# Output turned and stored by channel tiles behind the last down products, and the last activation tile made between additions

## The chip, the core and the metric

The kernel runs on one core of one Trainium2 chip. The core has five engines, each with an instruction stream of its own, tied to the others by semaphores: TensorE (PE) multiplies and transposes, with its results in PSUM; VectorE (DVE), ScalarE (ACT) and GpSimd (POOL) work on elements; SyncE (SP) issues transfers, which 16 DMA engines carry out. The metric is the device time of one execution in microseconds; lower is better.

## The reference

One inference step of one decoder layer for a prompt of 1024 tokens and for 8 decoding sequences of one token. An attention branch and a recurrent branch are merged and projected; then comes a SwiGLU mixer with a causal convolution of width 3 along the tokens. The end of the layer is what matters here:

```python
def conv_ffn(h, w_up, conv_w, conv_b, w_down, buf):
    u, v = jnp.split(h @ w_up, 2, axis=-1)
    u_ext = jnp.concatenate([buf.astype(u.dtype), u], axis=1)
    y = conv_b
    for j in range(CONV_W):
        y = y + conv_w[j] * u_ext[:, j:j + t]
    return (jax.nn.silu(y) * v) @ w_down, u_ext[:, -(CONV_W - 1):]
...
    f_out, conv_new = conv_ffn(h2, lw['w_up'], lw['conv_w'], lw['conv_b'], lw['w_down'], conv_buf0)
    x = x + g2[:, None, :] * f_out
    return x, nsa_new + (s_hg, conv_new)
```

The model width is 1024, the hidden width of the mixer 2816. `x` is the output y_prompt (1024 x 1024) and y_sample (8 x 1024); `conv_new` holds the last inputs of the convolution.

## The kernel before

The residual stream `xT` lies in SBUF with channels on the partitions: KT = 8 channel tiles of 128, each with 1032 columns (1024 prompt tokens, 8 decode tokens). The columns are worked in three chunks c of CH = 344. Each matrix product is split into three of shorter numbers (`product`, lines 245 to 247: high by high, high by low, low by high), so every chunk of one weight tile is three instructions.

`stage_ffn` runs over FT = 22 hidden tiles f, two at a time in GR = 11 groups g. In `body(g, ...)` TensorE makes the up products of the two tiles (u into PSUM banks 0 to 2, v into 3 to 5) and then the down products of the group before: for each channel tile n and chunk c six products into bank 6 or 7 in turn. VectorE convolves, multiplies by v and splits the activation tile (`hidden`: three multiplications, L3025; a cast, L235; a subtraction, L240), and adds each down chunk to `xT` (L3060, with the decode columns apart, L3058, when c is 2). The semaphore `added` counts these additions, and TensorE waits for it before it writes a bank again. In a group, VectorE does both convolutions, then the 24 additions, then the activation tile 2g + 1. The last call, `body(GR, ...)`, has down products alone; its weights were loaded into the ring and split before. Before it TensorE waits for `a_ready`, which `hidden` gives.

Behind the last addition TensorE turns the tails (22 tiles of 10 columns, L2951) by groups of four, VectorE copies them (L3080), and SP stores them as p_cf and s_cf. Then `stage_output` runs in a block of its own: per tile t of 128 tokens TensorE turns eight 128 x 128 pieces of `xT` (L3099), VectorE copies one half of the channels (L3108) and ScalarE the other (L3116) into one of two buffers in the ring, and SP stores 128 whole rows of 4096 bytes (L3124). A copy waits until the store of two tiles before has landed. Nothing plans this order: each engine follows the order in which its instructions are written.

Of the kernel before, what the change touches and what calls it, by code (L numbers as in the profile page):

```python
# [13 lines left out]
ALU = mybir.AluOpType  # L14
# [3 lines left out]
P = 128  # L18
D = 1024
# [2769 lines left out]
def stage_ffn(nc, s, T, mix, up_weights, norm):  # L2789
# [30 lines left out]
    x = s.xT  # L2820

# [12 lines left out]
    with nc.Block() as block:  # L2834
        @block.sync
        def _(sp):
# [16 lines left out]
            sp.wait_ge(copied, (FT + 3) // 4)  # L2853
            sp.dma_start(T["p_cf"][0, 0], rows[0:2, :]).then_inc(out, 16)
            sp.dma_start(T["s_cf"][0, :, 1], rows[2:2 + NB, :]).then_inc(out, 16)
            sp.wait_ge(out, 32)
# [32 lines left out]
        def _(pe):  # L2889
# [3 lines left out]
            def body(g, par, up, down):  # L2893
# [34 lines left out]
                if down:  # L2928
                    weights = wd if up else wd_last
                    pe.wait_ge(dn_split, g)  # L2930
                    pe.wait_ge(a_ready, 2 * g)
                    for n in range(KT):
                        for c in range(3):
# [3 lines left out]
                            for e in range(2):  # L2937
                                last = product(pe, s.ps[6 + (3 * n + c) % 2][:, 0:CH], [w[:, e, n * P:(n + 1) * P] for w in weights],
                                               (aH[1 - par][:, e, cols], aL[1 - par][:, e, cols]), e == 0, e == 1)
# [5 lines left out]
            body(GR, 1, False, True)  # L2945

            pe.wait_ge(added, 24 * GR + 2)
            for f in range(FT):
                if f % 4 == 0 and f >= 8:
                    pe.wait_ge(copied, f // 4 - 1)  # L2950
                last = pe.transpose(s.ps[6 + f // 4 % 2][0:NB + 2, (f % 4) * P:(f % 4 + 1) * P],  # L2951
                                    tails[:, f * 10:(f + 1) * 10], s.ident[:, :])
                if f % 4 == 3 or f == FT - 1:
                    last.then_inc(turned, 1)
# [33 lines left out]

        @block.vector
        def _(v):  # L2990
# [26 lines left out]

            def hidden(f, h, par):

                whole, hi, lo = (t[par][:, h, :] for t in (a, aH, aL))  # L3020
                v.wait_ge(silu_done, f + 1)
                for c in range(3):
                    cols = slice(c * CH, (c + 1) * CH)
                    v.wait_ge(v_made, 3 * f + c + 1)
                    last = v.tensor_tensor(whole[:, cols], y[:, cols], s.ps[3 + c][:, 0:CH], ALU.mult)  # L3025
                    if c < 2:
                        last.then_inc(v_read, 1)
                ch.link(v, last)
                v.nop().then_inc(v_read, 1)
                ch.link(v, high(v, hi, whole))  # L3030
                low(v, lo, whole, hi).then_inc(a_ready, 1)

            def body(g, par, up, down, more=True):
# [28 lines left out]
                if up:  # L3062
                    hidden(2 * g + 1, 1, par)
# [12 lines left out]
            ch.link(v, v.tensor_tensor(x[:, :, SEQ:TOK], x[:, :, SEQ:TOK], dec, ALU.add))  # L3076
            for g in range((FT + 3) // 4):
                n = min(4, FT - 4 * g) * P
                v.wait_ge(turned, g + 1)
                v.tensor_copy(rows[0:NB + 2, 512 * g:512 * g + n], s.ps[6 + g % 2][0:NB + 2, 0:n]).then_inc(copied, 1)  # L3080


def stage_output(nc, s, T):

    y = [view(s.ring, 1024 * i, D) for i in range(2)]
    turned, done = s.sem("o_turned"), [s.sem("o_done_v"), s.sem("o_done_a")]
    sent = [s.sem(f"o_sent{i}") for i in range(2)]

    with nc.Block() as block:
        @block.tensor  # L3090
        def _(pe):
            for t in range(TT + 1):
                n = rows_of(t)
                for half in range(2):
                    g = 2 * t + half

                    wait(pe, done[half], t - 3)
                    for j in range(4):
                        last = pe.transpose(s.ps[g % 8][0:n, j * P:(j + 1) * P],  # L3099
# [166 lines left out]
```

## Time and profile before

| | us |
|---|---|
| median of 3 runs | 2311.18 (2309.67 to 2312.91) |
| the profiled execution | 2305.29 |
| its span | 2303.5 |
| TensorE busy | 2156.0, 94% of the span |
| VectorE busy | 1190.4, 52% |
| ScalarE busy | 660.4, 29% |
| GpSimd busy | 590.7, 26% |

The profile is one execution, and its times are counted from the start of the span. The granted clock is TensorE's: 1.00 is its level of 2.4 GHz, 0.50 that of 1.2 GHz; its mean here is 0.965. A duration of a product is from its start to its modelled end, and products overlap, so the distance between starts is what one costs in a row of them.

### The profile page before, as it was taken

Reading aid. Unit: us, or ns where it says so; the run is one execution under the profiler, and the core shown is the slowest. Engines: PE = TensorE matmul, PEld = TensorE weight load, DVE = VectorE, ACT = ScalarE, POOL = GpSimd, SP = SyncE. Lnnn points to the kernel's source line nnn. Section 1 sums busy time; section 2 is a strip of 40 time slices with the busy share of each in tenths; the row PEclk is TensorE's granted clock in tenths of the full one; section 3 lists DMA queues with packets and bytes.
Section 4 is the critical chain, followed back from the end, with each engine's and each line's share of the span. In section 5 each row is a group of like instructions: output and inputs, shape, how many; then the busy total and the mean of one; then the engine's idle time right before and its main releaser. Section 6 shows DMA issues by size and latency. Waiting matters only on the chain. (4 is left out here: it accounts for less than half of the span.)

```text
span 2303.5 us, 34296 instructions
## 1 busy us (share of the span) xinstructions
PE 2156.0 (94%) x13481; PEld 1967.1 (85%) x13481; DVE 1190.4 (52%) x2152; ACT 660.4 (29%) x1390; POOL 590.7 (26%) x367
## 2 busy tenths in 40 slices
PE   8999997988869999987999999999999999999996
PEld 3798785666656799987999999899999999999996
DVE  5773465888857167763110333565445444445444
ACT  3332464776744034431111212331111101110100
POOL 0112113444631155541000114422221202221200
PEclk9999897999979999988999999999999999999998
DMA  9021452000026312211333443221111111111101
GB/s 363 25 77 34 130 177 88 1 1 1 1 79 229 115 28 57 57 47 48 87 87 83 149 136 86 73 57 56 56 37 54 39 51 41 52 41 48 45 19 76
DMA packets 168405, 168.83 MB, mean 73 GB/s; under 512 B 10178, under 2 KB 147811, under 8 KB 162932
## 3 DMA queue, kind: packets, MB, share of 16 engines
q1 hardware_dynamic: 160278, 118.16, 17.0%
q0 software_dynamic: 7760, 48.55, 6.3%
q8 instruction: 105, 1.72, 0.3%
q14 instruction: 38, 0.31, 0.0%
q10 hardware_dynamic: 224, 0.08, 0.0%
HBM read 153.19 MB, written 17.87 MB: 74 GB/s over the span
## 5 line engine op out<-in xcount | busy, mean ns | idle before, releaser
L245 PE MATMUL psall<-hT_short,ring_short 128*128 128x344 f32 x1896 | 613.1, 323 | 6.9 <-PEq L1843 5.7
L247 PE MATMUL psall<-hT_short,ring_short 128*128 128x344 f32 x1896 | 606.5, 320 | 0.0
L240 POOL TENSOR_TENSOR ring_short<-ring,ring_short 128x1024 fp32r<-128x1024 f32 (+3 forms) x53 | 201.4, 3802 | 1089.6 <-DVE ring_short L235 768.6
L246 PE MATMUL psall<-work_short,ring_short 128*128 128x344 f32 x1392 | 446.4, 321 | 0.0
L245 PEld LDWEIGHTS psall<-hT_short,ring_short 128*128 128x128 f32 x1896 | 357.5, 189 | 7.9 <-issue 6.8
L247 PEld LDWEIGHTS psall<-hT_short,ring_short 128*128 128x128 f32 x1896 | 357.4, 189 | 0.0
L246 PEld LDWEIGHTS psall<-work_short,ring_short 128*128 128x128 f32 x1392 | 263.0, 189 | 0.2
L3060 DVE SCALAR_TENSOR_TENSOR xT<-psall,mod,xT 128x344 f32<-128x344 f32 (+1 forms) x264 | 151.4, 573 | 129.7 <-PE psall L247 126.6
L246 PE MATMUL psall<-xT_short,ring_short 128*128 128x344 f32 x648 | 207.5, 320 | 0.0
L245 PE MATMUL psall<-work_short,work_short 128*128 128x344 f32 x528 | 176.3, 334 | 2.9 <-POOL work_short L240 2.9
L2971 ACT ACTIVATE work<-psall 128x344 f32<-128x344 f32 (+1 forms) x66 | 30.0, 456 | 503.9 <-PE psall L247 503.0
L246 PE MATMUL psall<-work_short,work_short 128*128 128x344 f32 x528 | 169.1, 320 | 0.0
L247 PE MATMUL psall<-work_short,work_short 128*128 128x344 f32 x528 | 168.9, 320 | 0.0
L235 DVE CAST ring_short<-ring 128x2048 fp32r<-128x2048 f32 (+3 forms) x44 | 49.6, 1127 | 183.0 <-DMA ring<-in_w_in 144.6
L1147 POOL TENSOR_SCALAR ring<-ring,work 128x640 f32<-128x640 f32 (+7 forms) x128 | 104.7, 824 | 97.7 <-DVE work L1345 96.4
L246 PEld LDWEIGHTS psall<-xT_short,ring_short 128*128 128x128 f32 x648 | 122.4, 189 | 0.0
L3008 DVE SCALAR_TENSOR_TENSOR work<-work,conv 128x1024 f32<-128x1024 f32 x22 | 42.8, 1948 | 149.7 <-ACT work L2982 149.7
L1360 DVE TENSOR_TENSOR work_short<-psall,work_short 128x512 fp32r<-128x512 f32 (+1 forms) x148 | 100.9, 685 | 33.5 <-ACT work_short L1283 31.2
L245 PEld LDWEIGHTS psall<-work_short,work_short 128*128 128x128 f32 x528 | 99.0, 188 | 17.8 <-DVE xT L3060 13.9
L1240 PE MATMUL psall<-work_short,work_short 128*128 128x512 f32 (+1 forms) x296 | 108.8, 450 | 0.0
L1283 ACT ACTIVATE work_short<-psall 128x512 fp32r<-128x512 f32 (+1 forms) x148 | 87.6, 594 | 69.1 <-PE psall L1223 42.2
L1223 PE MATMUL psall<-ident,ring 128*128 128x128 f32 x528 | 83.5, 282 | 17.8 <-POOL ring L1147 9.3
(445 smaller groups left out, 4031.7 us busy)
## 6 DMA issues: line engine op xcount, KB each, us to landing
ring<-in_w_up SPq DMA_DIRECT2D x44, 512.0 KB, 5.0
ring<-in_w_in SPq DMA_DIRECT2D x27, 512.0 KB, 5.1
work<-in_ada_w SPq DMA_DIRECT2D x23, 512.0 KB, 4.1
work<-in_w_down SPq DMA_DIRECT2D x10, 1024.0 KB, 4.9
ring<-in_ada_w SPq DMA_DIRECT2D x9, 512.0 KB, 4.4
x_spill<-xT SPq DMA_DIRECT2D x4, 1032.0 KB, 14.8
xT<-x_spill SPq DMA_DIRECT2D x4, 1032.0 KB, 7.4
ring<-in_ada_w SPq DMA_DIRECT2D x4, 1024.0 KB, 17.5
```

Source lines behind the costliest of these rows:

```text
L235: return eng.tensor_copy(hi, src)
L240: return eng.tensor_tensor(lo, src, hi, ALU.subtract)
L245: pe.matmul(out, w[0], x[0], start=first, stop=False)
L246: pe.matmul(out, w[0], x[1], start=False, stop=False)
L247: return pe.matmul(out, w[1], x[0], start=False, stop=last)
L1147: pool.tensor_scalar(p, p, recip[:, u.index % 4, j:j + 1], s.gates[:, u.t, column:column + 1], ALU.mult, ALU.mult).then_inc(normed, 1)
L1223: last = pe.transpose(turn_ps[i % 2][:, j * P:(j + 1) * P], probability(u, j)[:, (c - u.lo) * P:(c - u.lo + 1) * P], s.ident[:, :])
L1240: last = pe.matmul(out_ps[u.pair % 2], kept, split_T[i % 3][part][0:rows], start=(i == pair_first[u.pair] and part == 0), stop=(i == pair_ ...
L1283: act.activation(split_T[i % 3][0][0:rows], turn_ps[i % 2][0:rows, :], ACT.Copy).then_inc(high_done, 1)
L1360: v.tensor_tensor(lo, turn_ps[i % 2][0:rows, :], hi, ALU.subtract).then_inc(low_done, 1)
L3008: ch.link(v, v.scalar_tensor_tensor(out=y[:, 0:SEQ], in0=u[:, 1:SEQ + 1], scalar=taps[1], in1=y[:, 0:SEQ], op0=ALU.mult, op1=ALU.add))
L3060: v.scalar_tensor_tensor(out=at, in0=ps[:, 0:m], scalar=s.mod[:, G2 + n, 0:1], in1=at, op0=ALU.mult, op1=ALU.add).then_inc(added, 1)
```

## The change

In the last group with up products (`more` is false, g = 10), the five instructions of the last activation tile stand among the additions: a multiplication behind each addition of channel tile 2, the cast behind chunk 1 of tile 3, the subtraction behind chunk 1 of tile 4.

The last down products are written out. Behind the three chunks of channel tile n TensorE turns four tail tiles (n below 6, into bank 5) and all eight token pieces of channel tile n - 1 (into banks 0 and 1 or 2 and 3). ScalarE copies the tails and both halves of the output tile, into one of four buffers. SP stores one channel tile at a time: 128 partitions, 8 token tiles, 128 channels, which is 1024 pieces of 512 bytes. The last channel tile is copied by ScalarE and VectorE, a half each, and stored as two halves. The decode columns are turned, copied and stored last. `stage_output` is gone.

```diff
+    y_out = [view(s.ring, 4096 + 1024 * i, TT, P) for i in range(4)]
+    finished = lambda n: 24 * (GR - 1) + 3 * n + 5
+    def y_banks(n):
+        return s.psall[:, 1024 * (n % 2):1024 * (n % 2) + 1024].rearrange("p (t c) -> p t c", t=TT)
...
+            def send(n, tiles):
+                sp.dma_start(y_prompt[:, tiles, n * P:(n + 1) * P], y_out[n % 4][:, tiles, :]).then_inc(sent[n % 4], 16)
+
+            for n in range(KT - 1):
+                sp.wait_ge(y_copied, 2 * n + 2)
+                send(n, slice(0, TT))
+                if n == KT - 3:
+                    sp.wait_ge(copied, TURNS)
+                    sp.dma_start(T["p_cf"][0, 0], rows[0:2, :]).then_inc(out, 16)
+                    sp.dma_start(T["s_cf"][0, :, 1], rows[2:2 + NB, :]).then_inc(out, 16)
+            sp.wait_ge(y_copied, 2 * KT - 1)
+            send(KT - 1, slice(0, HALF))
+            sp.wait_ge(y_copied_v, 1)
+            send(KT - 1, slice(HALF, TT))
+            sp.wait_ge(dec_copied, 1)
+            sp.wait_ge(dec_copied_v, 1)
+            sp.dma_start(T["y_sample"][:, 0], y_dec).then_inc(out, 16)
...
-            body(GR, 1, False, True)
-
-            pe.wait_ge(added, 24 * GR + 2)
-            for f in range(FT):
...
+            def turn_output(n):
+                pe.wait_ge(added, finished(n))
+                wait(pe, y_copied, 2 * (n - 1))
+                for t in range(TT):
+                    last = pe.transpose(y_banks(n)[:, t, :], x[:, n, t * P:(t + 1) * P], s.ident[:, :])
+                    if t % HALF == HALF - 1:
+                        last.then_inc(y_turned, 1)
...
+            for n in range(KT):
+                for c in range(3):
...
+                    pe.wait_ge(added, 24 * (GR - 1) + 3 * n + c + 1)
...
+                if n < TURNS:
+                    turn_tails(n)
+                if n:
+                    turn_output(n - 1)
+            turn_output(KT - 1)
...
+            for n in range(KT):
+                last = pe.transpose(s.ps[4 + n // 4][0:NB, n % 4 * P:(n % 4 + 1) * P], x[:, n, SEQ:TOK], s.ident[:, :])
...
+            for n in range(KT):
+                if n < TURNS:
+                    copy_tails(n)
+                if n:
+                    wait(act, sent[(n - 1) % 4], 16 * ((n - 1) // 4))
+                    for half in range(2):
+                        copy_output(n - 1, half)
+            act.wait_ge(sent[3], 16)
+            copy_output(KT - 1, 0)
...
+                            if not more and n == 2:
+                                hide(2 * g + 1, 1, par, c)
+                            elif not more and (n, c) == (3, 1):
+                                hidden_high(1, par)
+                            elif not more and (n, c) == (4, 1):
+                                hidden_low(1, par)
-                if up:
+                if up and more:
                     hidden(2 * g + 1, 1, par)
...
+            v.wait_ge(y_turned, 2 * KT)
+            v.wait_ge(sent[3], 16)
+            v.tensor_copy(y_out[3][:, HALF:TT, :], y_banks(KT - 1)[:, HALF:TT, :]).then_inc(y_copied_v, 1)
...
-def stage_output(nc, s, T):
...
-    stage_output(nc, s, T)
```

On VectorE, at the end of group 9's additions in `body(10, ...)`, before: the last three additions (L3058 and L3060), the activation tile (L3025, L235, L240), and the first additions of the last group.

```order
L3060 SCALAR_TENSOR_TENSOR xT<-psall,mod,xT 128x344 x2
L3058 TENSOR_TENSOR work<-work,psall 128x8
L3060 SCALAR_TENSOR_TENSOR xT<-psall,mod,xT 128x336
L3025 TENSOR_TENSOR work<-work,psall 128x344 x3
L235 CAST work_short_2064_12211<-work 128x1032
L240 TENSOR_TENSOR work_short_2064_12213<-work,work_short_2064_12211 128x1032
L3060 SCALAR_TENSOR_TENSOR xT<-psall,mod,xT 128x344 x2
```

The same place of the changed kernel, from the first multiplication on, behind the addition of chunk (2, 0); additions are L3144 and L3142, the multiplication is L3098.

```order
L3098 TENSOR_TENSOR work<-work,psall 128x344
L3144 SCALAR_TENSOR_TENSOR xT<-psall,mod,xT 128x344
L3098 TENSOR_TENSOR work<-work,psall 128x344
L3142 TENSOR_TENSOR work<-work,psall 128x8
L3144 SCALAR_TENSOR_TENSOR xT<-psall,mod,xT 128x336
L3098 TENSOR_TENSOR work<-work,psall 128x344
L3144 SCALAR_TENSOR_TENSOR xT<-psall,mod,xT 128x344 x2
L235 CAST work_short_2064_12211<-work 128x1032
L3142 TENSOR_TENSOR work<-work,psall 128x8
L3144 SCALAR_TENSOR_TENSOR xT<-psall,mod,xT 128x336
L3144 SCALAR_TENSOR_TENSOR xT<-psall,mod,xT 128x344 x2
L240 TENSOR_TENSOR work_short_2064_12213<-work,work_short_2064_12211 128x1032
```

The five instructions have moved from behind the 24 additions to between them; the first of them stands behind the seventh addition.

On TensorE, at one channel tile of the last down products (the difference, with n between 1 and 4): L2975 turns tails, L2983 turns the output.

```order
 L247 MATMUL psall<-work_short_2064_12211,ring_short_2048_9730 128x344
+L2975 MATMUL psall<-ident,work 10x128 x4
+L2983 MATMUL psall<-ident,xT 128x128 x8
 L245 MATMUL psall<-work_short_2064_12211,ring_short_2048_9728 128x344
 L246 MATMUL psall<-work_short_2064_12213,ring_short_2048_9728 128x344
```

And on TensorE at the end of the program.

```order
 L246 MATMUL psall<-work_short_2064_12213,ring_short_2048_9728 128x344
 L247 MATMUL psall<-work_short_2064_12211,ring_short_2048_9730 128x344
-L2951 MATMUL psall<-ident,work 10x128 x22
-L2834 UNCONDITIONAL_BRANCH
-L3090 UNCONDITIONAL_BRANCH
-L3099 MATMUL psall<-ident,xT 128x128 x64
-L3099 MATMUL psall<-ident,xT 8x128 x8
-L3089 UNCONDITIONAL_BRANCH
+L2983 MATMUL psall<-ident,xT 128x128 x16
+L3005 MATMUL psall<-ident,xT 8x128 x8
+L2844 UNCONDITIONAL_BRANCH
```

All 22 tail transposes and 48 of the 64 output transposes have moved ahead of the last product; 16 output transposes and the eight of the decode columns stand behind it, and the second block is gone.

## Rows read from the trace of the kernel before

**Rows 1.** The chain of waits that ended last, 2283 to the end; start us, us, what

```profile
2283.13 8.86 PE psall L3099 x60
...
2292.74 4.21 DMA out_y_prompt<-ring
...
2297.76 2.73 DMA out_y_prompt<-ring
```

**Rows 2.** Busy time by stretch; length, then busy us (instructions) per engine, clock, DMA

```profile
2243.00:2247.40 4.40, 0.12 (x1) 0.02 (x1) 3.93 (x7) 0.00 (x0) 0.00 (x0) 0.90 0.00 2
2247.40:2253.30 5.90, 5.89 (x21) 5.90 (x22) 1.47 (x4) 0.00 (x0) 0.00 (x0) 0.50 0.00 0
2274.00:2279.00 5.00, 3.32 (x23) 1.52 (x22) 4.32 (x9) 0.00 (x0) 0.00 (x0) 1.00 0.00 0
2277.00:2303.50 26.50, 11.90 (x83) 10.32 (x82) 8.50 (x13) 5.37 (x9) 0.00 (x0) 0.76 0.43 164
```

**Rows 3.** Timeline around the wait ahead of the last down products; start, length, engine

```profile
2242.80 0.32 PE L247 MATMUL psall<-work_short,work_short 128*128 128x344 f32 x1
...
2243.84 1.35 DVE L3025 TENSOR_TENSOR work<-work,psall 128x344 f32<-128x344 f32 x3
2245.34 0.70 DVE L235 CAST work_short<-work 128x1032 fp32r<-128x1032 f32 x1 [0.16 <-DVE work L3025]
2246.08 1.23 DVE L240 TENSOR_TENSOR work_short<-work,work_short 128x1032 fp32r<-128x1032 f32 x1
...
2247.41 0.63 PE L245 MATMUL psall<-work_short,ring_short 128*128 128x344 f32 x1 [4.29 <-DVE work_short L240]
```

**Rows 4.** Timeline, one period of the last additions, DVE and PE

```profile
2256.85 0.42 PE L245 MATMUL psall<-work_short,ring_short 128*128 128x344 f32 x1
...
2257.90 0.32 PE L245 MATMUL psall<-work_short,ring_short 128*128 128x344 f32 x1
...
2258.10 0.57 DVE L3060 SCALAR_TENSOR_TENSOR xT<-psall,mod,xT 128x344 f32<-128x344 f32 x1 [0.55 <-PE psall L247]
...
2258.85 0.32 PE L245 MATMUL psall<-work_short,ring_short 128*128 128x344 f32 x1
...
2259.05 0.17 DVE L3058 TENSOR_TENSOR work<-work,psall 128x8 f32<-128x8 f32 x1 [0.37 <-PE psall L247]
...
2259.25 0.57 DVE L3060 SCALAR_TENSOR_TENSOR xT<-psall,mod,xT 128x336 f32<-128x336 f32 x1
...
2259.87 0.43 PE L245 MATMUL psall<-work_short,ring_short 128*128 128x344 f32 x1
```

**Rows 5.** Busy time by stretch of 1 us inside the output stage's transposes

```profile
2286.00:2287.00 1.00, 1.00 (x7) 1.00 (x6) 0.65 (x1) 0.19 (x1) 0.00 (x0) 0.50 0.38 156
...
2288.00:2289.00 1.00, 1.00 (x12) 1.00 (x11) 0.44 (x1) 0.44 (x1) 0.00 (x0) 1.00 0.70 283
```

**Rows 6.** Timeline, the tail transposes of L2951 on PE

```profile
2274.96 1.04 PE L2951 MATMUL psall<-ident,work 128*10 128x128 f32 x8 [0.86 <-DVE xT L3060]
2276.41 1.20 PE L2951 MATMUL psall<-ident,work 128*10 128x128 f32 x8 [0.41 <-DVE work L3080]
```

**Rows 7.** Timeline on PE, transposes (L637) between products of another stage

```profile
123.28 0.34 PE L247 MATMUL psall<-ring_short,xT_short 128*128 128x384 f32 x1
123.55 0.41 PE L637 MATMUL psall<-ident,work 8*128 8x8 f32 x4
```

**Rows 8.** Timeline, the last copies and the last store's issue (SPq)

```profile
2299.30 0.60 ACT L3116 ACTIVATE ring<-psall 128x512 f32<-128x512 f32 x1 [1.67 <-DMA out_y_prompt<-ring]
2299.31 0.69 DVE L3108 COPY ring<-psall 128x512 f32<-128x512 f32 x1 [1.57 <-DMA out_y_prompt<-ring]
...
2301.29 0.30 SPq L3124 DMA_DIRECT2D out_y_sample<-ring  x1
```

**Rows 9.** GB/s in 40 slices, 866 to 876; then 2285 to 2303.5

```profile
GB/s 0 0 0 0 0 0 0 0 0 0 0 131 311 295 279 279 279 279 295 213 0 0 0 33 111 197 281 346 344 348 334 105 0 0 0 0 0 0 0 33
...
GB/s 0 0 0 204 416 407 106 337 416 381 0 399 425 310 124 425 399 151 213 399 425 98 27 27 18 0 124 407 407 399 416 390 124 0 319 381 425 80 0 0
```

More of the change, by code:

```diff
@@ L2851, in _ @@
             sp.dma_start(raw_last, w_dn[:, 2 * GR - 2:2 * GR, :]).then_inc(last_in, 16)
[L2853 to L2856, printed above, removed]
+            y_prompt = T["y_prompt"][0].rearrange("(t p) c -> p t c", p=P)
+            def send(n, tiles):
[14 more added lines that the diff above has]
+            sp.dma_start(T["y_sample"][:, 0], y_dec).then_inc(out, 16)
+            for b in range(4):
+                sp.wait_ge(sent[b], 48 if b == 3 else 32)
+            sp.wait_ge(out, 48)
         @block.gpsimd
@@ L2937, in body @@
                             for e in range(2):
-                                last = product(pe, s.ps[6 + (3 * n + c) % 2][:, 0:CH], [w[:, e, n * P:(n + 1) * P] for w in weights],
+                                last = product(pe, s.ps[6 + (3 * n + c) % 2][:, 0:CH], [w[:, e, n * P:(n + 1) * P] for w in wd],
                                                (aH[1 - par][:, e, cols], aL[1 - par][:, e, cols]), e == 0, e == 1)
@@ L2987, in _, with copy_tails, copy_output @@
             groups(act, body, 8, ch)
+            def copy_tails(q):
+                act.wait_ge(turned, q + 1)
+                cols = slice(512 * q, min(512 * q + 512, DFF))
+                act.activation(rows[0:NB + 2, cols], s.ps[5][0:NB + 2, 0:cols.stop - cols.start], ACT.Copy).then_inc(copied, 1)
+            def copy_output(n, half):
+                act.wait_ge(y_turned, 2 * n + half + 1)
+                tiles = slice(HALF * half, HALF * half + HALF)
+                act.activation(y_out[n % 4][:, tiles, :], y_banks(n)[:, tiles, :], ACT.Copy).then_inc(y_copied, 1)
+            for n in range(KT):
[7 more added lines that the diff above has]
+            copy_output(KT - 1, 0)
+            act.wait_ge(dec_turned, 1)
+            act.activation(y_dec[:, 0:512], s.ps[4][0:NB, :], ACT.Copy).then_inc(dec_copied, 1)
         @block.vector
@@ L3075, in _ @@
             ch.link(v, v.tensor_tensor(dec, dec, s.mod[:, G2:G2 + KT, 1:NB + 1], ALU.mult))
[L3076 to L3080, printed above, removed]
-def stage_output(nc, s, T):
[L3085 to L3099, printed above, removed]
-                                            s.xT[:, 4 * half + j, t * P:t * P + n], s.ident[:, :])
-                    last.then_inc(turned, 1)
-        def copy_half(eng, copy, half):
-            for t in range(TT + 1):
-                n = rows_of(t)
-                eng.wait_ge(turned, 2 * t + half + 1)
-                wait(eng, sent[t % 2], 16 * (t // 2))
-                copy(y[t % 2][0:n, 512 * half:512 * (half + 1)], s.ps[(2 * t + half) % 8][0:n, :]).then_inc(done[half], 1)
-        @block.vector
-        def _(v):
-            copy_half(v, v.tensor_copy, 0)
-        @block.scalar
-        def _(act):
-            copy_half(act, lambda o, i: act.activation(o, i, ACT.Copy), 1)
-        @block.sync
-        def _(sp):
-            for t in range(TT + 1):
-                for half in range(2):
-                    sp.wait_ge(done[half], t + 1)
-                dst = T["y_prompt"][0, t * P:(t + 1) * P] if t < TT else T["y_sample"][:, 0]
-                sp.dma_start(dst, y[t % 2][0:rows_of(t), :]).then_inc(sent[t % 2], 16)
-            for b in range(2):
-                sp.wait_ge(sent[b], 16 * len(range(b, TT + 1, 2)))
```

61 lines of the change are left out of this document (43 added, 18 removed).

## The prediction

> **What bounds the kernel now.** I read the chain of waits at the end first, then the busy time by stage, then the timeline of the two places where the stages show a waiting TensorE. The chain [rows 1] runs through 8.86 us of TensorE transposes of the output stage and, behind them, through stores of y_prompt: DMA 4.21 us, a copy, DMA 2.73 us, a copy. Nothing but output work stands in the last 20 us. The stages [rows 2] say the same: from 2277.00 to 2303.50 TensorE is busy 11.90 of 26.50 us, and it starts the transposes at half clock (0.50). Two output buffers alternate, so a copy waits until the store of two tiles ago has landed (2.73 us in the chain). The second place is ahead of the last down products: from 2243.00 to 2247.40 TensorE does 0.12 us of work. The timeline [rows 3] shows why. Group 9's last product starts at 2242.80 and, at 0.16 us a product, ends at 2242.96; VectorE then makes the last activation tile (three multiplications, a cast, a subtraction, up to 2247.31) and only then does TensorE go on, at 2247.41. The granted clock falls with it: 21 products start in 2247.40 to 2253.30 at 0.50, the 1.2 GHz level.
>
> **Part one: the last activation tile between additions.** Its inputs are ready (its v products are older than the additions), so all that counts is how far five extra VectorE instructions delay additions that TensorE waits for; the down products use two PSUM banks. One period of additions [rows 4]: a chunk of six products takes 0.95 us, or 1.05 behind a wait; VectorE starts 0.20 us behind a chunk's end, adds in 0.58 us (0.77 with the decode columns of c = 2), and TensorE restarts 0.05 us behind an addition. A period of three chunks is 3.02 us (2256.85 to 2259.87) with one small wait. I set the end of chunk (n, c) = (2, 0) to 0 and walk on. Additions and multiplications (0.48 each, from 1.35 for three [rows 3], rounded up):
> (2,0) added 0.78, multiplied 1.28; (2,1) ends 1.13, added 1.91, multiplied 2.41; (2,2) ends 2.08, added 3.20, multiplied 3.73; (3,0) ends 3.03, added 4.33; (3,1) has to wait for 3.20, ends 4.30; (3,2) waits for 4.33, ends 5.43; (3,1) added 5.08, cast 0.70 to 5.84; (3,2) added 6.63; (4,0) ends 6.38, added 7.23; (4,1) waits for 6.63, ends 7.73, added 8.51; subtraction 1.23 to 9.76; (4,2) ends 8.68, added 10.55; (5,0) ends 9.63; (5,1) waits for 10.55, ends 11.65. Undisturbed, (5,1) ends at 10.19. The delay is 1.46 us. Bounds: 0, if the idle VectorE time held everything, and 3.28 us (1.35 + 0.70 + 1.23), if nothing were hidden. I take 1.46.
> So group 9 ends at 2242.96 + 1.46 = 2244.42 rather than 2247.41 (3.0 us gained), and without a stop of over 4 us I expect the clock to stay at 1.00: 21 products at 0.158 us are 3.3 us rather than the 5.9 us of [rows 2], 2.6 us gained.
>
> **Part two: the last down products with the tails and the transposes among them.** Per channel tile n TensorE now does three chunks, four tail transposes (n < 6) and the eight output transposes of n - 1. Cadence of a transpose: a window of 1 us at clock 1.00 touches 12 of them, each 0.273 us long, so (1 + 0.273)/12 = 0.106 us [rows 5]; the eight tail transposes of [rows 6] give (1.04 - 0.27)/7 = 0.11. At half clock the window touches 7. A change between products and transposes: the four small ones at 123.55 start 0.27 us behind a product of 384 columns, which by its width takes 384/344 of 0.158 = 0.18 [rows 7], so some 0.1 us each way. Bounds for a pair 0 and 0.4, I take 0.2.
> Until chunk (7,2) ends: 24 chunks 22.75, the first wait 0.2, 22 tail transposes 2.4, six output turns of 8 at 0.106, 5.1, seven interruptions 1.4: 31.85 us. The small waits for additions of [rows 4] vanish, since the transposes give VectorE about 1 us more. ScalarE's copies (0.60 us for 512 columns [rows 8], so 1.8 us per tile) fit into a step of 4.1 us. So (7,2) ends at 2244.42 + 31.85 = 2276.27.
> Stores: each step has to store 512 KB, now in pieces of 512 bytes at a row pitch of 4096, where the old stores had whole rows of 4096 bytes. The nearest row for 512-byte stores is out_s_hg, 512 KB: its slices stand at 279 to 311 GB/s (the first line of [rows 9]); I take 280, 1.9 us per tile. Bounds: the 416 GB/s that a slice of the old stores reached [rows 9] is the best (1.3 us), and the worst I set below as a rival. 1.9 us are hidden in steps of 4.1. The issue on SP costs some 0.3 us (y_sample's took 0.30 [rows 8]) and SP has nothing else to do. It passes six stores before p_cf and s_cf, and nobody waits for those two but the end.
>
> **The end.** Turn 6 follows (7,2): 2277.2. Turn 7 needs the addition of (7,2): 2276.27 + 0.20 + 0.77 + 0.05 = 2277.3, then 0.85 to 2278.15, its results visible some 0.2 later. ScalarE: tile 6 copied at 2278.2, half of 7 at 2278.8; VectorE: the other half, 0.69 us, at 2279.2. The decode transposes follow, 0.9 us, and their copies end near 2280.0. SP sends tile 6 at 2278.2, the halves of tile 7 at 2278.85 and 2279.3, y_sample at 2280.0. From the old y_sample store's issue to the span's end it was 2.2 us [rows 8], so the end is at least 2282.2. The three y_prompt stores are 1 MB, 3.75 us at 280 GB/s; the fixed part is what the 2.73 us of [rows 1] leave beside about 1.3 us of data, 1.4 us; 2278.2 + 1.4 + 3.75 + 0.1 = 2283.45. The later one decides: 2283.5, against 2303.5. The block change between the two stages and its 4 us go too; they are inside that difference.
> **Sum:** 20.0 us off the profiled execution's 2305.29, or 2285.3. The median of the runs shown is 5.9 us above the profiled execution; on that median, which a new measurement is compared with, it is 2311.2 - 20.0 = **2291 us**.
>
> **The rivals.**
> 1. The clock. Here the transposes are a quarter to a third of TensorE's time from 2244 on, and the last 2.6 us hold nothing else. The trace speaks against harm: during pure transposes the clock rose from 0.50 (2286) to 1.00 (2288) [rows 5]. Closing stretch alone at half clock: 24 transposes at 0.2 rather than 0.106, 2.3 us more, 2293. All of the last stage at half clock: 144 products at 0.281 (5.9/21) rather than 0.158, 17.7 us, and 94 transposes 9 us, so 27 - 20 = 7 us slower, 2318.
> The Trainium skill says in "TensorE: Matmul & The Clock Gate", Part 4: PE-mode transpose, that the full clock does not engage for transpose mode, since it does not count as TensorE activity in the same way. By that rule the closing stretch, or the whole stage, would be the case of this rival. The trace disagrees where it can be seen: the clock rose under transposes alone.
> 2. The stores become the bound. If a store of 512-byte pieces takes T per tile and T is over 4.1 us, they queue. The first is sent near 2253.1 (two steps and two copies behind 2244.4) and the last lands at 2253.1 + 1.4 + 8T. At T = 5.2 (100 GB/s) this is 2296, 7 us faster than before, 2304. It decides against the change from T = 6.1 us on (85 GB/s); at T = 7 the end is 2310.5, 7 us slower, 2318. This is the case on the other side: one place (the DMA queue of the last stage), one price (8 times what T exceeds). For it: 512-byte pieces at a pitch that no store of the trace has, eight times as many descriptors as before. Against it: out_s_hg in [rows 9] had 512-byte pieces as well and ran at about 280.
> 3. The inserted instructions make TensorE stop so that the clock falls all the same. Three waits of 0.1 to 1 us rather than one of 4.3; in the tail before, gaps of 0.86 and 0.41 us [rows 6] left the clock at 1.00 (2274 to 2279 [rows 2]). If it fell, the 2.6 us stay unsaved and the delay grows to the 3.28 bound: 15.6 us faster, 2295.6.
> 4. The change moves the work but the end comes from the same stores: that would need T near 6, so it is the middle of rival 2.
>
> **How the numbers follow.** Forecast (gain of 16 to 24 us) 0.80; closing stretch at half clock 0.05; rival 3 0.05; store queue with T of 4.5 to 5.6 us 0.04; T near 6, no change 0.03; T above that, or the clock half throughout, 0.03. A measurement of this kernel can tell 0.2%, 4.6 us, from no change. Faster 0.94, within 0.03, slower 0.03. The range: downward the insertion hidden (1.5), switches free (1.4), the store at full speed (1.3) and the base itself, whose three runs spread over 3 us and which stands 5.9 above the profiled execution: 2284. Upward the insertion unhidden (1.8), switches doubled (1.4), a closing half clock (2.3) and slower closing stores, 2 to 3 us: 2299.
>
> **What would show it.** In the changed kernel's profile: no TensorE gap ahead of the last down products, waits of up to 1 us at three places in group 9's additions; clock 1.00 from there to the last transpose; steps near 4.1 us per channel tile; TensorE's last transpose near 2279; stores of 512 KB landing in 3.5 to 4.5 us each, never two in flight before the last three; last DMA some 4 us behind TensorE's last output transpose. I am wrong if stores pile up (the copies on ScalarE waiting for a landed store), if TensorE waits for ScalarE's copies in the last stage, or if the clock reads 0.50 inside it.

## The result and the profile after

| | before | after |
|---|---|---|
| median of 4 runs, us | 2311.95 (2309.67 to 2312.91) | 2292.09 (2289.63 to 2292.89) |
| profiled execution, us | 2305.29 | 2291.57 |
| its span, us | 2303.5 | 2288.5 |
| its mean granted clock | 0.965 | 0.968 |

The ratio after to before is 0.9917, with an interval from 0.9900 to 0.9934. The median before is that of the three runs shown ahead and one more. The forecast was 2291 us; the medians differ by 19.9 us, and 20.0 had been worked out. The two spans differ by only 15.0 us. That is no contradiction. The first product of group 9's down products starts at 2218.95 in the profiled execution before and at 2225.29 in the one after, although the work ahead of it is the same. Over all profiled executions of this study that start lies between 2218.95 and 2233.66. So I compare traces from this product on. From there to the span's end it was 84.55 us before, and it is 63.21 after: 21.3 us less.

The busy time by stretch of the kernel before, cut at the end of group 9's down products, at the start and at the end of the last down products. (The columns are length, then busy us and instructions of PE, PEld, DVE, ACT and POOL, then the clock, DMA share and GB/s.)

```profile
2218.95:2242.96 24.01, 24.01 (x146) 22.41 (x144) 14.33 (x30) 0.00 (x0) 0.00 (x0) 1.00 0.00 1
2242.96:2247.41 4.45, 0.16 (x1) 0.03 (x1) 3.93 (x7) 0.00 (x0) 0.00 (x0) 0.90 0.00 2
2247.41:2273.94 26.53, 26.53 (x144) 25.16 (x144) 14.33 (x30) 0.00 (x0) 0.00 (x0) 0.89 0.00 1
2273.94:2303.50 29.56, 13.69 (x96) 11.21 (x94) 10.96 (x19) 5.37 (x9) 0.00 (x0) 0.79 0.39 147
```

The same view of the kernel after. The stretch of the stop no longer exists.

```profile
2225.29:2250.23 24.94, 24.35 (x146) 22.42 (x145) 17.09 (x35) 0.00 (x0) 0.00 (x0) 1.00 0.00 1
2250.23:2280.78 30.55, 30.55 (x217) 29.58 (x216) 15.06 (x32) 9.30 (x18) 0.00 (x0) 1.00 0.33 96
2280.78:2288.50 7.72, 2.98 (x25) 2.31 (x23) 2.55 (x6) 2.26 (x4) 0.00 (x0) 0.91 0.70 186
```

Group 9 became 0.93 us longer, the stop of 4.45 us is gone, the last down products became 4.02 us longer although they now hold 70 transposes, and what stands behind them shrank from 29.56 to 7.72 us: -0.93 + 4.45 - 4.02 + 21.84 = 21.3 us. The clock column answers to [rows 2]: where 21 products had started at 0.50, it now reads 1.00.

Where [rows 3] showed VectorE's block of five instructions and a TensorE wait of 4.29 us, these instructions now stand between additions. In the timeline, the second half of that place is the one at which TensorE waits longest.

```profile
2240.24 1.22 DVE L240 TENSOR_TENSOR work_short<-work,work_short 128x1032 fp32r<-128x1032 f32 x1
...
2241.28 0.32 PE L247 MATMUL psall<-work_short,work_short 128*128 128x344 f32 x1
2241.38 0.15 DVE L3142 TENSOR_TENSOR work<-work,psall 128x8 f32<-128x8 f32 x1
2241.57 1.05 DVE L3144 SCALAR_TENSOR_TENSOR xT<-psall,mod,xT 128x336 f32<-128x336 f32 x2
...
2242.20 0.43 PE L245 MATMUL psall<-work_short,work_short 128*128 128x344 f32 x1 [0.59 <-DVE xT L3144]
```

The subtraction (L240) holds VectorE for 1.22 us, the addition of a c = 2 chunk stands behind it, and TensorE waits for that addition. Its last product takes 0.16 us from 2241.28, so the wait is 2242.20 - 2241.44 = 0.76 us.

One channel tile of the last down products on TensorE, timeline:

```profile
2256.36 0.32 PE L247 MATMUL psall<-work_short,ring_short 128*128 128x344 f32 x1
2256.52 0.60 PE L2975 MATMUL psall<-ident,work 128*10 128x128 f32 x4
2256.95 1.04 PE L2983 MATMUL psall<-ident,xT 128*128 128x128 f32 x8
2257.74 0.40 PE L245 MATMUL psall<-work_short,ring_short 128*128 128x344 f32 x1
2257.99 0.32 PE L246 MATMUL psall<-work_short,ring_short 128*128 128x344 f32 x1
...
2260.67 0.60 PE L2975 MATMUL psall<-ident,work 128*10 128x128 f32 x4
```

The tails begin 0.16 us behind the last product's start, which is a product's own time, so the change of kind cost nothing there. For the change back the product behind the transposes has to be counted too, since its own distance is 0.25 us rather than 0.16. From 2256.36 to 2257.99 there are 1.63 us; two products at 0.158 and 12 transposes at 0.109 (the price that e4 gives below) are 1.62. A pair of changes costs 0.01 us here. A step, from one group of tails to the next, is 4.15 us.

The end of the program, timeline of TensorE, ScalarE, VectorE and SP's queue:

```profile
2280.77 2.11 PE L2983 MATMUL psall<-ident,xT 128*128 128x128 f32 x16
2281.47 1.68 ACT L3050 ACTIVATE ring<-psall 128x512 f32<-128x512 f32 x3 [2.63 <-PE psall L2983]
2282.58 2.30 SPq L2866 DMA_DIRECT2D out_y_prompt<-ring  x3
2282.72 1.04 PE L3005 MATMUL psall<-ident,xT 128*8 128x128 f32 x8
2283.80 0.68 DVE L3171 COPY work<-psall 8x512 f32<-8x512 f32 x1 [0.18 <-PE psall L3005]
2284.98 0.77 SPq L2881 DMA_DIRECT2D out_y_sample<-work  x1
```

Sixteen output transposes and the eight of the decode columns are all that is left behind the products, as against the 8.86 us of [rows 1]. What comes last is y_sample: it is issued at 2284.98, right behind the issues of the last y_prompt pieces, for 0.77 us, where in [rows 8] it took 0.30, and the span ends 3.52 us behind that issue's start, where it was 2.2 in [rows 8]. SP's waits for the landings, in their order (us in total, times, longest):

```profile
SPq L2883 <- DMA out_y_prompt<-ring: 1.9, 1, 1.9
SPq L2884 <- DMA out_y_sample<-work: 0.4, 1, 0.4
```

The last y_prompt piece has landed at 2284.98 + 0.77 + 1.9 = 2287.6, and y_sample lands behind it.

The nine y_prompt stores by their line (times of the issue min/median/max in ns, first and last issue; then the landing), and GB/s in 40 slices from 2257 to the end:

```profile
L2866 SPq DMA_DIRECT2D out_y_prompt<-ring x9: 372/383/1231, 2258.7 to 2283.6; - x9
...
DMA to landing us min/median/max: 3.2/3.3/4.0
```
```profile
GB/s 0 0 0 177 291 198 0 0 101 288 272 25 0 25 294 291 55 0 0 237 290 139 0 0 223 291 152 0 14 292 288 187 29 89 287 291 285 287 133 0
```

The full slices stand at 285 to 294 GB/s. Before each of the first six stores there are slices of zero: each has landed before the next starts. The old stores had reached 416 to 425 GB/s [rows 9], so the new form is slower by a third, and it does not matter, since a step leaves it 4.15 us.

### The profile page after: what moved, and what is told of

Same layout as the page of the kernel before. It is cut to its first block, busy times and chain, and to the rows that moved or that the text cites. A ratio compares the mean times of both kernels' runs of the same rounds, so it can differ in the third digit from the quotient of the medians.

```text
span 2288.5 us, 34276 instructions
## 1 busy us (share of the span) xinstructions
PE 2153.0 (94%) x13481; PEld 1964.6 (86%) x13481; DVE 1180.2 (52%) x2139; ACT 666.6 (29%) x1403; POOL 590.9 (26%) x367
## 4 chain that ended last, share of the span: by engine, by line
PE 51%; DVE 1%; ACT 0%; POOL 0%; issue 0%; ACTq 0%
PE psall L245 17%; PE psall L247 16%; PE psall L246 16%; PE psall L2549 2%; DVE work L2413 1%; DVE work_short L2425 0%; PE psall L2983 0%; DVE xT L2710 0%; PE psall L2975 0%; DVE xT L2717 0%; PE psall L2394 0%; PE psall L2395 0%; PE psall L2619 0%; DVE xT L3144 0%; DVE work_short L240 0%; POOL work L2387 0%
## 5 line engine op out<-in xcount | busy, mean ns | idle before, releaser
L240 POOL TENSOR_TENSOR ring_short<-ring,ring_short 128x1024 fp32r<-128x1024 f32 (+3 forms) x53 | 201.7, 3807 | 1092.3 <-DVE ring_short L235 771.8
L3144 DVE SCALAR_TENSOR_TENSOR xT<-psall,mod,xT 128x344 f32<-128x344 f32 (+1 forms) x264 | 151.3, 573 | 132.8 <-PE psall L247 129.2
L235 DVE CAST ring_short<-ring 128x2048 fp32r<-128x2048 f32 (+3 forms) x44 | 49.5, 1126 | 180.4 <-DMA ring<-in_w_in 144.2
```

The lines of the kernel that those rows point to most:

```text
L235: return eng.tensor_copy(hi, src)
L240: return eng.tensor_tensor(lo, src, hi, ALU.subtract)
L3144: v.scalar_tensor_tensor(out=at, in0=ps[:, 0:m], scalar=s.mod[:, G2 + n, 0:1], in1=at, op0=ALU.mult, op1=ALU.add).then_inc(added, 1)
```

## The experiments

Start and end of each stretch are taken from the same products in every profile (us):

| kernel | group 9 | stop | last down products | closing | total |
|---|---|---|---|---|---|
| before | 24.01 | 4.45 | 26.53 | 29.56 | 84.55 |
| after | 24.94 | 0 | 30.55 | 7.72 | 63.21 |
| e1_part_one | 24.95 | 0 | 24.13 | 29.44 | 78.52 |
| e2_part_two | 23.97 | 4.46 | 33.14 | 7.78 | 69.35 |
| e3_stores_x3 | 24.95 | 0 | 30.56 | 25.63 | 81.14 |
| e4_more_turns | 24.93 | 0 | 30.51 | 13.01 | 68.45 |
| e5_no_tile | 23.98 | 0.64 | 30.41 | 7.70 | 62.73 |
| e7_closing | 24.94 | 0 | 32.69 | 7.16 | 64.78 |
| e8_spread | 23.98 | 0 | 32.69 | 5.92 | 62.59 |
| after_again | 24.95 | 0 | 30.56 | 7.78 | 63.29 |
| e9_best | 23.99 | 0 | 31.39 | 6.71 | 62.09 |
| after_third | 24.95 | 0 | 30.56 | 7.73 | 63.24 |

A stretch repeats within 0.1 us from execution to execution (the three rows of after), far closer than whole times do. That is why small effects are read from this table. The closing stretches of e7, e8 and e9 are an exception, told with e9.

**Part one alone** (before, with the tile made between additions):

```diff
+                            if not more and n == 2:
+                                hide(2 * g + 1, 1, par, c)
+                            elif not more and (n, c) == (3, 1):
+                                hidden_high(1, par)
+                            elif not more and (n, c) == (4, 1):
+                                hidden_low(1, par)
-                if up:
+                if up and more:
                     hidden(2 * g + 1, 1, par)
```

> Part one alone: the last activation tile is made between additions, the tails and the output stage stay as they were. My theory: TensorE's 4.45 us stop ahead of the last down products goes, the additions of group 9 are late by 0.9 us (as in the changed kernel's profile, not the 1.46 of the prediction), and the half clock stretch of 21 products (2.6 us) goes: 4.45 - 0.93 + 2.6 = 6.1 us faster, some 2306. Rival: the clock falls all the same because of the small waits, then 3.5 us faster. Second rival: the two parts need each other and alone this one gives nothing.

Measured: 2301.87 us (7 runs) against 2308.22 (10), 6.35 us less, ratio 0.9976 (0.9965 to 0.9988). From group 9 on it gains 84.55 - 78.52 = 6.03 us. Busy time by stretch, the last down products and what follows:

```profile
2250.53:2274.66 24.13, 24.13 (x146) 22.41 (x144) 15.06 (x32) 0.00 (x0) 0.00 (x0) 1.00 0.00 1
2274.66:2304.10 29.44, 13.35 (x96) 10.77 (x94) 10.96 (x19) 5.37 (x9) 0.00 (x0) 0.83 0.39 148
```

The clock reads 1.00 and the products take 24.13 rather than 26.53 us, and the end is untouched. So part one gives about 6 us: 4.45 of the stop and 2.40 of the clock, less 0.94 of delay.

**Part two alone** (after, with the tile made behind the additions again):

```diff
-                            if not more and n == 2:
-                                hide(2 * g + 1, 1, par, c)
-                            elif not more and (n, c) == (3, 1):
-                                hidden_high(1, par)
-                            elif not more and (n, c) == (4, 1):
-                                hidden_low(1, par)
-                if up and more:
+                if up:
                     hidden(2 * g + 1, 1, par)
```

> Part two alone: the output is turned and stored by channel tiles, the last activation tile stays behind the 24 additions. My theory: the stop of 4.4 us and the half clock behind it come back, all else is as in the changed kernel: 6 us slower than that, 14 us faster than before, some 2298; the half clock stretch lasts about 6 us as before, though four to twelve of its instructions are now transposes. Rival: transposes do not count as activity, so the clock stays at 0.50 longer than the 6 us of before, and the gain falls below 12 us.

Measured: 2296.08 us (4 runs), 12.1 us less than the 2308.22 beside it, ratio 0.9948 (0.9931 to 0.9965); from group 9 on 15.2 us less. The two gains add up: 6.0 + 15.2 = 21.2, and after has 21.3 (by the medians 6.4 + 12.1 = 18.5, where after has 18.8 to 20.7). Busy time by stretch, from the stop on:

```profile
2248.72:2253.10 4.38, 0.16 (x2) 0.00 (x0) 3.93 (x7) 0.00 (x0) 0.00 (x0) 0.90 0.00 2
2253.10:2259.00 5.90, 5.83 (x21) 5.54 (x22) 1.41 (x4) 0.00 (x0) 0.00 (x0) 0.50 0.00 0
2259.00:2286.32 27.32, 27.32 (x195) 26.54 (x194) 12.93 (x27) 9.29 (x18) 0.00 (x0) 1.00 0.37 107
```

The stop brings 5.90 us at 0.50 again, as in [rows 2]. The transposes between the products do not call it up later: the clock is 1.00 from 2259.00 to the last product. Whether they lengthen it is hardly tried here, since all but the last three of the 21 instructions at 0.50 are products; [rows 5] shows the clock rise under transposes alone. Part two was taken away only as a whole: how its 15.2 us divide between the transposes moved ahead, the four buffers and the block change that is gone (TensorE stood still for 4.37 us there) is not shown.

**Three times the stores** (each piece of y_prompt is also written to two spare tensors in HBM, with waits to match; the result itself is complete):

```diff
                 sp.dma_start(y_prompt[:, tiles, n * P:(n + 1) * P], y_out[n % 4][:, tiles, :]).then_inc(sent[n % 4], 16)
+                for spare in (T["spare0"], T["spare1"]):
+                    sp.dma_start(spare[:, tiles, n * P:(n + 1) * P], y_out[n % 4][:, tiles, :]).then_inc(sent[n % 4], 16)
```

> Every y_prompt tile is stored three times, twice into spare memory of the same shape, so 1.5 MB per channel tile. My theory: stores of 512-byte pieces run at some 286 GB/s and cost nothing while a tile's stores take less than the 4.1 us step; three times 1.83 us is 5.5, so they queue: from the first issue (2258.7 in the changed kernel) 1.4 + 8 x 5.5 us, an end some 16 us later than the changed kernel's, its closing stretch a DMA busy without a gap. Rival: the DMA queue has more room than one tile's rate shows and the end moves by less than 5 us. Second rival: the issue on SP (24 issues) or ScalarE's four buffers bind first, and TensorE is held up in the last stage.

Measured, one run: 2311.54 us, closing stretch 25.63 rather than 7.72, 17.9 us more; the store theory had said 16. GB/s in 40 slices from 2260 to the end, and the y_prompt stores by their line (issue min/median/max in ns):

```profile
GB/s 0 229 281 279 287 277 281 285 280 289 286 286 276 293 277 275 292 280 285 283 279 278 286 280 281 286 278 288 305 235 286 306 299 291 277 268 285 288 154 9
```
```profile
L2866 SPq DMA_DIRECT2D out_y_prompt<-ring x9: 378/1737/2751, 2260.5 to 2301.8; - x9
```

There is no gap in the transfers; the busy time of 2262 to 2282 puts them at 283 GB/s, beside a TensorE at 1.00 that is never idle:

```profile
2262.00:2282.00 20.00, 20.00 (x145) 19.47 (x145) 9.30 (x21) 7.18 (x14) 0.00 (x0) 1.00 1.01 283
```

So 1.57 MB per tile takes 5.5 us against a step of 4.15: T is over the step, and the excess, with the three times larger last tiles, comes out at the end. TensorE was not held up (30.56 us of last down products), and ScalarE waited 0.2 us in all for a store, so its four buffers did not bind. Nor did the issues on SP: they last longer here than the 0.38 us of after, but the rate of 283 GB/s is close to the 285 to 294 of a single store's full slices. That is the rival of the store queue with its mechanism at work, and it also shows how far after is from it: T is a third of 5.5, 1.8 us.

**Sixty-four more transposes** behind the last output turn, into banks that are not read:

```diff
             turn_output(KT - 1)
+            for n in range(KT):
+                for t in range(TT):
+                    pe.transpose(s.ps[6 + t // 4][:, t % 4 * P:(t % 4 + 1) * P], x[:, n, t * P:(t + 1) * P], s.ident[:, :])
```

> 64 further output transposes, whose results nobody reads, stand behind the last output turn and ahead of the decode transposes. My theory: transposes keep TensorE's clock at 1.00, each costs 0.108 us, TensorE's part is 6.9 us longer, and the end some 5.2 us later (y_sample's store no longer waits behind those of y_prompt). Rival: transposes do not hold the clock, it falls to 0.50 within the added stretch, and part of them cost 0.21 us: 8 to 12 us later.

Measured, one run: 2292.11 us; the closing stretch is 5.29 us longer. TensorE's timeline and, below it, the busy time of the stretch of the added transposes:

```profile
2277.20 2.11 PE L2983 MATMUL psall<-ident,xT 128*128 128x128 f32 x16
2279.14 7.15 PE L3004 MATMUL psall<-ident,xT 128*128 128x128 f32 x64
2286.13 1.04 PE L3008 MATMUL psall<-ident,xT 128*8 128x128 f32 x8
```
```profile
2279.10:2286.00 6.90, 6.90 (x65) 6.90 (x64) 0.69 (x1) 0.47 (x1) 0.00 (x0) 1.00 0.53 152
```

Eighty transposes in a row stand at 1.00 to their end, at (2286.13 - 2279.14)/64 = 0.109 us each. They cost only 5.29 of their 6.98 us, since y_sample no longer stands behind the y_prompt stores: it is issued 6.57 us later, not 6.98, and the span ends 2.24 us behind its issue rather than 3.52.

**Without the tile** (the five instructions left out; the last down products read what lies there):

```diff
-                            if not more and n == 2:
-                                hide(2 * g + 1, 1, par, c)
-                            elif not more and (n, c) == (3, 1):
-                                hidden_high(1, par)
-                            elif not more and (n, c) == (4, 1):
-                                hidden_low(1, par)
                 if up and more:
                     hidden(2 * g + 1, 1, par)
+                elif up:
+                    v.sem_inc(v_read, 3)
+                    v.sem_inc(a_ready, 1)
```

> The changed kernel without the last activation tile: its five VectorE instructions are left out, and the last down products read what lies there. My theory: the 24 additions of group 9 then have the old period of 3.02 us, and the distance from the first addition of group 9 to the last down products is 0.9 us shorter than in the changed kernel; the rest is unchanged. Rival: the 0.9 us are in something else (the bank waits of the products), and the distance stays within 0.2 us.

Measured, one run: 2294.19 us, and group 9 takes 23.98 rather than 24.94 us. The insertion delays the additions by 0.96 us, not by 1.46. The 0.64 us of stop come from the edit: the signal for the last tile stands behind all 24 additions, so TensorE waits for the last of these.

**A shorter closing, first try** (transposes between chunks 1 and 2 of a tile rather than behind chunk 2, the first half of the last tile turned before the last addition, y_sample issued by ScalarE; the cut shows the first of the three):

```diff
                     last.then_inc(d_made, 1)
-                if n < TURNS:
-                    turn_tails(n)
-                if n:
-                    turn_output(n - 1)
+                    if c == 1:
+                        if n < TURNS:
+                            turn_tails(n)
+                        if n:
+                            turn_output(n - 1)
```

> The changed kernel with another closing: tails and output tile n - 1 are turned behind chunk 1 of channel tile n rather than behind chunk 2, the first half of the last tile is turned before the last addition, and y_sample is issued on ScalarE's queue. My theory: tile 6's store starts 1.9 to 2.8 us earlier, so the closing stretch from the last product's end to the span's end falls from 7.7 us to some 5.5. Rival: the end is set by the last half tile's own chain (addition, turn, copy, store), which does not move, and less than 1 us is gained.

Measured, one run: 2291.24 us. The closing stretch is 0.56 us shorter and the last down products are 2.14 us longer. Of these, 0.87 are the turn of tile 6 (eight transposes), which now stands ahead of the last product instead of behind it. The other 1.27 are a wait that is back. The timeline at one channel tile:

```profile
2253.11 0.16 DVE L3143 TENSOR_TENSOR work<-work,psall 128x8 f32<-128x8 f32 x1 [0.81 <-PE psall L247]
2253.31 0.57 DVE L3145 SCALAR_TENSOR_TENSOR xT<-psall,mod,xT 128x336 f32<-128x336 f32 x1
2253.71 0.32 PE L247 MATMUL psall<-work_short,ring_short 128*128 128x344 f32 x1
2253.94 0.19 PEld L245 LDWEIGHTS psall<-work_short,ring_short 128*128 128x128 f32 x1 [0.20 <-DVE xT L3145]
2253.94 0.43 PE L245 MATMUL psall<-work_short,ring_short 128*128 128x344 f32 x1
2254.20 0.32 PE L246 MATMUL psall<-work_short,ring_short 128*128 128x344 f32 x1
```

Chunk 2's result takes two additions, 0.77 us together. Two chunks on, TensorE needs its bank and waits, as it did in [rows 4]: 2253.71 to 2254.20 are 0.49 us where two products take 0.32, so about 0.18 us in each of seven tiles. In after the transposes stand just behind chunk 2 and give VectorE that time. This was overlooked when the place was chosen.

**The same, with the tile spread out** (one small VectorE piece per channel tile, behind its chunk 0; `piece` multiplies for n = 0 to 2, casts for 3, subtracts for 4 to 6 and signals for 7):

```diff
-                            if not more and n == 2:
-                                hide(2 * g + 1, 1, par, c)
-                            elif not more and (n, c) == (3, 1):
-                                hidden_high(1, par)
-                            elif not more and (n, c) == (4, 1):
-                                hidden_low(1, par)
+                            if not more and c == 0:
+                                piece(2 * g + 1, 1, par, n)
```

> As e7_closing, and the last activation tile in seven pieces, one behind the addition of chunk 0 of each channel tile (three multiplications, one cast, three subtractions of 344 columns), where VectorE was idle for 0.55 us. My theory: at most 0.2 us of delay is left, so 0.7 us beside the 2.2 of the closing: 2.5 to 3 us faster than the changed kernel, 23 faster than before. Rival: the waits come from the seventh addition's bank and remain, then only the closing's gain is seen.

Measured: 2289.59 us (6 runs) against 2310.09, ratio 0.9900 (0.9876 to 0.9923). Busy time by stretch, group 9 and the last down products:

```profile
2224.71:2248.70 23.99, 23.99 (x147) 22.43 (x145) 17.37 (x37) 0.00 (x0) 0.00 (x0) 1.00 0.00 1
2248.70:2281.40 32.70, 32.70 (x224) 30.35 (x224) 15.07 (x32) 10.39 (x20) 0.00 (x0) 1.00 0.36 100
```

The delay of group 9 is gone (23.99, as without the tile); the last down products are as in e7.

**The kernel after once more**, beside e8:

> The changed kernel once more, on the same chip and in the same rounds as e8_spread. Expected: 0.9917 of before, as measured first, with the same stretch of 62.0 us from group 9's first addition to the end.

Measured: 2291.33 us (6 runs), ratio 0.9909 (0.9889 to 0.9928). e8 has 1.7 us less by the medians and 0.70 by the stretches, where 2.5 to 3 had been expected; the intervals overlap.

**The pieces spread, and the transposes behind chunk 2 again** (only tile 6 is turned between chunks 1 and 2 of the last tile):

```diff
-                    if c == 1:
-                        if n < TURNS:
-                            turn_tails(n)
-                        if n:
-                            turn_output(n - 1)
+                    if n == KT - 1 and c == 1:
+                        turn_output(n - 1)
+                if n < TURNS:
+                    turn_tails(n)
+                if 0 < n < KT - 1:
+                    turn_output(n - 1)
```

> As e8_spread, but the tails and output tiles stand behind chunk 2 again, as in the changed kernel; at the last channel tile alone output tile 6 is turned behind chunk 1. My theory: the transposes behind chunk 2 give VectorE the time for its longest addition (chunk 2 with the decode columns), and this is what e7 and e8 lost, 2.1 us over the last down products (0.27 a tile). So the last down products are 31.4 us (30.55 and one turn of 0.87 more) rather than 32.7, group 9 stays at 24.0, the closing near 5.9: 61.3 us from group 9's first product to the end, 1.9 less than the changed kernel's 63.2. Rival: the loss of e7 and e8 is the number of switches between products and transposes, which stays, and the last down products remain near 33 us.

Measured: 2288.63 us (4 runs) against 2310.61, ratio 0.9905 (0.9888 to 0.9922). Busy time by stretch:

```profile
2223.51:2247.50 23.99, 23.99 (x146) 22.45 (x145) 17.36 (x37) 0.00 (x0) 0.00 (x0) 1.00 0.00 1
2247.50:2278.89 31.39, 31.39 (x224) 30.39 (x223) 15.06 (x32) 10.38 (x20) 0.00 (x0) 1.00 0.37 103
2278.89:2285.60 6.71, 2.24 (x18) 1.41 (x15) 2.56 (x6) 1.18 (x2) 0.00 (x0) 0.98 0.62 169
```

The last down products are 1.30 us shorter than in e8, and 31.39 is after's 30.56 and the 0.87 of the turn of tile 6. So the place behind chunk 1 had cost 1.3 us, and not the 2.1 of the expectation, which counted the turn as a loss and then added it again. The closing was expected near 5.9 us and is 6.71.

The closing holds the same instructions in e7, e8 and e9, at the same distances: y_sample is issued 3.47 us behind the last product's end in all three. Yet it takes 7.16, 5.92 and 6.71 us. What differs is SP's wait for the last y_prompt pieces to land, here in this order:

```profile
SPq L2880 <- DMA out_y_prompt<-ring: 3.8, 1, 3.8
SPq L2880 <- DMA out_y_prompt<-ring: 2.2, 1, 2.2
SPq L2880 <- DMA out_y_prompt<-ring: 3.1, 1, 3.1
```

Why is open, and with one trace of each these three totals are known to 1.2 us only. The 0.70 us between e8 and after is inside that. e9's 62.09 us, the shortest total, would be 61.3 with the closing of e8 and 62.5 with that of e7; after has 63.2 or 63.3 each time.

**The kernel after a third time**, beside e9:

> The changed kernel beside e9_best, in the same rounds. Expected: 63.2 us from group 9's first product to the end again, and a median 1.9 us above that of e9_best, less than its own spread of some 4 us.

Measured: 2289.90 us (4 runs), ratio 0.9904 (0.9887 to 0.9920). By the stretches e9 is 1.15 us shorter than after (0.7 to 1.9, by what was said of its closing); by the medians 1.3 us, which these runs can't tell from nothing.

## Why the prediction was right

- **What bounds.** Both places read from [rows 1] and [rows 3] were the bounds. Each could be taken away alone (e1, e2), and the two gains add up.
- **Stop and half clock.** The stop went whole (4.45 us). The prediction has 2.6 us for the clock; e1 shows 26.53 - 24.13 = 2.40. Shown by e1 from one side, and by e2, where stop and half clock come back together, from the other.
- **The delay of group 9.** Worked out 1.46 us, measured 0.93 to 0.97, and 0.96 against the kernel without the tile. The walk added VectorE's instructions end to end, but they overlap: an addition or multiplication begins some 0.1 us before the one ahead has ended. Waits stand at three places, of 0.10, 0.15 and 0.76 us, as named. Right mechanism, size half too large.
- **The last down products.** Worked out 31.85 us, measured 30.55. The missing 1.3 us are the 1.4 set for seven changes between products and transposes. The range had held 0 to 0.4 for a pair, and 0 is right here; the 0.1 us that the prediction read off [rows 7] as a change did not show between these products and these transposes. Without the term it is 22.75 + 0.2 + 2.4 + 5.1 = 30.45.
- **The stores.** 280 GB/s assumed, 285 to 294 measured; landing 3.5 to 4.5 us assumed, 3.2 to 4.0 measured, never two in flight before the last ones. With T tripled (e3) they bound the end by 17.9 us, where the formula of the rival gave 16.
- **The closing.** Worked out 7.23 us, measured 7.72 (0.5 more), and here the path was wrong. The prediction let the y_prompt stores decide: 5.25 us from tile 6's issue to their landing, and it was 5.05 (2282.58 to 2287.63). The end was y_sample's. It was to be issued 3.73 us behind the last product and land 2.2 later; it was issued after 4.20 (SP was busy with the issues ahead, which took up to 1.23 us where 0.3 was set) and the span ended 3.52 behind that. With the y_prompt stores landed before (e4) it is 2.24 again.
- **The sum.** Group 9 0.5 and the changes 1.3 to the good, the closing 0.5 to the bad: 20.0 + 0.5 + 1.3 - 0.5 = 21.3, as in the traces. The clock's 2.6 us are no term of the forecast's end, which counts all 24 chunks at 1.00, so their being 2.4 changes nothing in it. By the medians it is 19.9 us, and 18.8 and 20.7 in the two repeats; they carry the whole times' own scatter of some 3 us. That the first lies within 0.1 us of the forecast's 20.0 is luck; in the traces the terms miss by 1.8 us one way and 0.5 the other.

The rivals. The clock (1) is refuted for this kernel: transposes among products leave it at 1.00 (e2, after), and 80 in a row as well (e4). Waits of up to 0.76 us (3) did not lower it either. The store queue (2) is a real mechanism that had no hold at T = 1.8 us. No change (4) would have wanted T near 6.

The Trainium skill says in "TensorE: Matmul & The Clock Gate", Part 4: PE-mode transpose, that the full clock does not engage for transposes. The granted clock in the rows of e4 reads 1.00 through 6.90 us that hold fp32 transposes alone. Here the measurement decides against the page; by it, and by the prediction's estimate, the closing stretch would have been 2.3 us longer.

## What to carry to other kernels

A stage that only turns and sends its results belongs among the products of the stage ahead, one tile behind them, as long as a tile's store takes less than a tile's step; compare these two numbers first. Within a tile, put the foreign TensorE work just behind the chunk whose reader is slowest: the same transposes one chunk earlier cost 1.3 us here. When a piece of work moves from one stretch to the next, take its own time out of the comparison first (0.87 us of e7's 2.14). A small edit is measured from a fixed instruction near it, not from the start of the program: the way to there varied by 14.7 us, the whole behind it by 0.1 in three traces of after. That has to be shown for each kernel, though: in e7 to e9 SP's wait for the last landing alone varied by 1.6 us.

## What the runs showed of the hardware that was not expected

- A change between fp32r products and fp32 transposes on TensorE costs 0.01 us a pair in after (1.63 us for two products and 12 transposes); a transpose of 128x128 takes 0.109 us at full clock in a row of 64.
- The issue of a DMA on SP depends on what is queued: 0.37 to 0.39 us for most stores of after, but 1.23 for the last half, and 1.74 median, up to 2.75, where the stores never pause (e3). y_sample's issue took 0.77 us behind three stores in flight, and 0.30 when they had landed (e4, below) or when it was issued by ScalarE beside them (e7, e8, e9):

```profile
2287.96 0.30 SPq L2881 DMA_DIRECT2D out_y_sample<-work  x1
```

- Stores of 512-byte pieces ran at 285 to 294 GB/s in after and at 283 back to back (e3), and a 512 KB store of them landed in 3.2 us at best; the old ones, of whole rows of 4096 bytes, had reached 425 GB/s [rows 9].
- VectorE's instructions overlap at their ends: in after a multiplication starts at 2232.79 where the addition ahead of it, from 2232.30 for 0.58 us, ends at 2232.88. A walk along its queue should use the distances of starts, not lengths.
